# A latent attention layer: scaling on ScalarE, values absorbed, and a maximum in three ranges

## The chip, the cores and the metric

The kernel runs on one core of a Trainium2 chip. The metric is the device time of one execution in microseconds (us), as the median of the runs. TensorE multiplies, VectorE, ScalarE and GpSimd compute on tiles, SyncE (SP) issues DMAs. All order between them is made by semaphores that the kernel writes out by hand.

## The reference, cut to what matters

Two layers on 1024 tokens of width 1024. The change touches the mixer of the first, attention with a latent key and value of 128:

```
cq  = rmsnorm(h @ w_dq)                 # 1024 x 384
ckv = rmsnorm([h_ctx; h] @ w_dkv)       # 1280 x 128, 256 context rows first
q_nope, q_rope = cq @ w_uq              # 8 heads, 128 and 64 wide
k_nope, v      = ckv @ w_ukv            # 8 heads, 128 and 128 wide
k = [k_nope, rope(kr)];  q = [q_nope, rope(q_rope)]
p = softmax(q @ k.T / sqrt(192))        # per head 1024 x 1280
o = p @ v                               # per head 1024 x 128
y = o @ w_o
```

Both layers go on with a gated ConvFFN, and the second mixer is a Conformer convolution. All of it is float32.

## The kernel before, in words

Activations lie transposed, features in the partitions. A float32 product is made of three products of float32r parts: `three()` (L2061) multiplies low by high, high by low and high by high into one PSUM bank. So each operand is first split: ScalarE copies the value into a high part, VectorE subtracts this from the value to get the low part. Transposes and the folds of the rotary part are plain float32.

Attention runs in half-steps n = 0 to 17, two to a head: even n takes the first 512 queries of head n/2, odd n the others. A half-step has four query blocks s = 0 to 3 of 128 queries. For each, TensorE makes the scores against 1280 keys (`scores()`, fifteen products into PSUM banks 0 to 2, in the key ranges 512, 512 and 256 of `KP`), VectorE the maximum over 1280 columns and its negation (`maxes()`, L1582 and L1583), ScalarE the exponential with the row sum (`exps()`, L968), and VectorE the reciprocal and the scaling of the row of 1280 (`scales()`, L1589 and L1590). The next scores wait for `s_free`, which the exponential raises, as there is one set of score banks.

Behind each block of scores TensorE works on something else, by lists. `TURNS` gives the ten key blocks of the half-step before that are transposed (four transposes each, L2278; ScalarE and VectorE make high and low parts, `tp_copy` and `tp_sub`), `WEIGHS` the ten key blocks whose transposed probabilities are multiplied by the values (three products of 512 columns each, summed in bank 5), one half-step later still for the last three. `PIECES_AT` gives the pieces of the projections for a coming half-step: query parts ("q", nine products of 512), rotary parts ("qr", nine and two float32 folds), keys ("k", three products a range) and values ("v", three products of 128 columns for each key block, so 24 behind s = 2 and six behind s = 3 of an even half-step). Pieces take turns in banks 6 and 7; `pj_done` and `pj_free` count them, ten to a head.

Weights come by SP's queue in units of 128 x 1024, one a head: 768 columns for the queries, 128 for the keys, 128 for the values. In the second block of an even half-step ScalarE and VectorE split the next head's unit (`head_unit()`, L1577 on VectorE), VectorE before the maximum of the third block. When bank 5 is complete, ScalarE copies the head's 512 outputs to `OST` and issues a DMA of them to memory (`out_copy()`, L984). Later `heads_back()` (L1020) loads them again as input of the output projection; the last head's is loaded, and the third weight unit split, only when its store has landed. GpSimd sums the modulation vectors of the later sub-layers meanwhile, and TensorE finishes them with one-column products (L2097) behind the first scores of an even half-step, into bank 7.

n = 0, 1 and 14 to 17 are written out, n = 2 to 13 are a loop of three trips. n = 16 and 17 have no scores: they transpose and weigh what is left. Each engine's queue runs in the order in which `step()` issues it; nothing is reordered.

## Time and profile before

| | us |
|---|---|
| median of 3 runs (range) | 2547.52 (2545.29 to 2552.27) |
| the profiled execution | 2544.82 |
| its span in the trace | 2543.0 |
| TensorE busy | 2480.3 |
| VectorE busy | 1883.2 |
| ScalarE busy | 1150.0 |
| GpSimd busy | 933.3 |

The profile is of one execution. A row gives where an instruction begins (us from the span's start), how long it is busy, and, in brackets, how long its engine sat idle before it and what ended that. Matmuls are pipelined: the duration of one is longer than the distance to the next, so distances between starts are what count on TensorE, and rows that merge several instructions can hold waits. L numbers are lines of the kernel. Attention's half-steps lie between 139 and 672 us.

### The profile page before, as it was taken

The page shows a single profiled execution, that of the slowest core. Times are in us where ns is not written, and L with a number is a line of the kernel's source. Part 1 is how long each engine was busy: PE and PEld are TensorE (multiplying, and loading weights), DVE is VectorE, ACT ScalarE, POOL GpSimd, SP SyncE. Part 2 cuts the span into 40 slices and gives each one's busy share as a digit, 9 for nine tenths or more (in the row PEclk, how much of TensorE's full clock was granted, in tenths as well). Part 3 has the DMA queues.
Part 4 walks back from the last instruction along what each step waited for, and adds up shares of the span by engine and source line. Part 5 has one row for each costly group of instructions (what it writes and reads, how often), then busy time and mean ns, then how long its engine had stood idle before and what let it go on. Part 6 is the DMA issues. An engine that isn't in the chain of part 4 may idle for free.

```text
span 2543.0 us, 31195 instructions
## 1 busy us (share of the span) xinstructions
PE 2480.3 (98%) x11410; PEld 1998.7 (79%) x11410; DVE 1883.2 (74%) x2164; ACT 1150.0 (45%) x1821; POOL 933.3 (37%) x611
## 2 busy tenths in 40 slices
PE   7989999999899999999999999999999999999998
PEld 3868888888687788888888887756877888888876
DVE  5467776766547999999537379997689999994352
ACT  3334444444543555555435342235545555554331
POOL 0068685850043566564002010000445756630001
PEclk9999999999999999999999999999999999999999
DMA  6134333320431222223536320011212222236362
GB/s 264 35 108 133 100 116 107 124 82 17 173 109 58 76 83 79 88 83 108 203 115 199 113 92 34 34 46 54 100 59 78 80 91 84 76 107 224 125 198 75
DMA packets 101988, 262.38 MB, mean 103 GB/s; under 512 B 11104, under 2 KB 12384, under 8 KB 101856
## 3 DMA queue, kind: packets, MB, share of 16 engines
q1 hardware_dynamic: 86448, 209.65, 24.2%
q0 software_dynamic: 11520, 41.95, 5.1%
q10 hardware_dynamic: 3888, 9.05, 1.0%
q8 instruction: 80, 1.31, 0.2%
q14 instruction: 52, 0.43, 0.1%
HBM read 216.56 MB, written 44.04 MB: 102 GB/s over the span
## 4 chain that ended last, share of the span: by engine, by line
PE 79%; DVE 15%; issue 2%; DMA 1%; ACT 1%; POOL 0%; SPq 0%; POOLq 0%; ACTq 0%; DVEq 0%
PE psum L2064 24%; PE psum L2066 23%; PE psum L2065 23%; DVE acts L1974 3%; DVE acts L1976 3%; PE psum L2278 2%; PE psum L2268 1%; PE psum L2267 1%; DVE weights_f32r L1671 1%; DVE acts L1978 1%; PE psum L2097 1%; DMA low<-x_t 1%; DVE high_f32r L1792 1%; DVE small L1582 1%; PE psum L2364 1%
## 5 line engine op out<-in xcount | busy, mean ns | idle before, releaser
L2064 PE MATMUL psum<-acts_f32r,weights_f32r 128*128 128x512 f32 x1728 | 683.4, 396 | 10.5 <-DVE acts_f32r L1458 3.0
L2066 PE MATMUL psum<-acts_f32r,weights_f32r 128*128 128x512 f32 x1728 | 674.2, 390 | 0.0
L2065 PE MATMUL psum<-acts_f32r,weights_f32r 128*128 128x512 f32 x1728 | 674.0, 390 | 0.0
L761 POOL TENSOR_TENSOR low<-low 128x512 f32<-128x512 f32 x91 | 132.2, 1453 | 992.1 <-ACT low L1063 987.3
L844 ACT ACTIVATE weights_f32r<-low 128x512 fp32r<-128x512 f32 (+1 forms) x494 | 324.6, 666 | 334.1 <-PE psum L2066 242.1
L2064 PEld LDWEIGHTS psum<-acts_f32r,weights_f32r 128*128 128x128 f32 x1728 | 325.2, 188 | 81.3 <-issue 6.0
L1804 DVE TENSOR_TENSOR weights_f32r<-low,weights_f32r 128x512 fp32r<-128x512 f32 x264 | 380.1, 1484 | 0.1
L2066 PEld LDWEIGHTS psum<-acts_f32r,weights_f32r 128*128 128x128 f32 x1728 | 325.2, 188 | 68.8
L2065 PEld LDWEIGHTS psum<-acts_f32r,weights_f32r 128*128 128x128 f32 x1728 | 325.5, 188 | 67.9 <-issue 2.2
L1811 DVE TENSOR_TENSOR weights_f32r<-low,weights_f32r 128x512 fp32r<-128x512 f32 x176 | 125.6, 719 | 235.0 <-ACT weights_f32r L844 232.2
L788 POOL TENSOR_TENSOR low<-low 128x512 f32<-128x512 f32 x150 | 265.8, 1772 | 39.8 <-DVE acts_f32r L1789 29.3
L844 ACT ACTIVATE low<-psum 128x512 f32<-128x512 f32 (+2 forms) x246 | 147.6, 600 | 172.4 <-PE psum L2066 159.8
L2064 PE MATMUL psum<-high_f32r,weights_f32r 128*128 128x512 f32 (+1 forms) x464 | 184.5, 398 | 4.5 <-ACT low L844 4.5
L844 ACT ACTIVATE weights_f32r<-psum 128x512 fp32r<-128x512 f32 x160 | 92.9, 596 | 205.7 <-PE psum L2278 205.7
L2066 PE MATMUL psum<-high_f32r,weights_f32r 128*128 128x512 f32 (+1 forms) x464 | 179.2, 386 | 0.0
L2065 PE MATMUL psum<-high_f32r,weights_f32r 128*128 128x512 f32 (+1 forms) x464 | 179.2, 386 | 0.0
L811 POOL TENSOR_TENSOR low<-low 128x512 f32<-128x512 f32 x38 | 60.5, 1591 | 249.9 <-ACT low L844 249.9
L2064 PE MATMUL psum<-acts_f32r,high_f32r 128*128 128x256 f32 (+1 forms) x336 | 135.7, 404 | 10.8 <-ACT low L968 8.7
L1582 DVE TENSOR_REDUCE small<-psum 128x1 f32<-128x1280 f32 x64 | 95.3, 1490 | 60.4 <-PE psum L2268 60.0
L1156 ACT ACTIVATE low<-low,vectors 128x1024 f32<-128x1024 f32 x76 | 94.5, 1246 | 76.8 <-DVE low L1875 55.9
L738 POOL TENSOR_TENSOR set<-set 128x1024 f32<-128x1024 f32 x49 | 124.1, 2532 | 4.1
L2065 PE MATMUL psum<-acts_f32r,high_f32r 128*128 128x256 f32 (+1 forms) x336 | 125.3, 373 | 0.0
(240 smaller groups left out, 4646.7 us busy)
## 6 DMA issues: line engine op xcount, KB each, us to landing
low<-units SPq DMA_DIRECT2D x130, 512.0 KB, 4.1
low<-units SPq DMA_DIRECT2D x176, 256.0 KB, 3.5
set<-mod_w POOLq DMA_DIRECT2D x80, 512.0 KB, 3.9
gated<-low SPq DMA_DIRECT2D x44, 512.0 KB, 2.6
low<-gated SPq DMA_DIRECT2D x88, 256.0 KB, 4.0
residual<-low SPq DMA_DIRECT2D x48, 256.0 KB, 2.0
acts<-mod_w SPq DMA_DIRECT2D x4, 1024.0 KB, 8.9
low<-x_t SPq DMA_DIRECT2D x4, 1024.0 KB, 17.8
```

What stands on the lines that cost most here:

```text
L738: add = pool.tensor_tensor(acc, acc, part, ADD)
L761: pool.tensor_tensor(acc, first, ring(n), ADD).then_inc(sq_added, 1)
L788: pool.tensor_tensor(f(to[part - 1], HALF), x, y, op).then_inc(s_new, 1)
L844: return act.activation(out, in_, ACT.Copy, scale=scale)
L1156: act.activation(f(at), src, ACT.Identity, scale=V[:, wv + 2 * FB + c:wv + 2 * FB + c + 1], bias=V[:, wb + c:wb + c + 1]).then_inc(tap_mid, 1)
L1582: chain(dve.reduce_max(S[:, C_MX + c:C_MX + c + 1], PS[:, 0:KEYS], AX.X))
L1804: dve.tensor_tensor(r(at + HALF, HALF), src, r(at, HALF), SUB).then_inc(w_lo, 1)
L1811: dve.tensor_tensor(r(at + HALF, HALF), dn_raw(layer, dn_item(turn, j)), r(at, HALF), SUB).then_inc(w_lo, 1)
L1974: chain.lag(dve.scalar_tensor_tensor(out=into, in0=UE[i % 2][:, j:j + HALF + 1], scalar=tap(2 * j, i), in1=into, op0=MUL, op1=ADD))
L2064: pe.matmul(out, wl, xh, start=first, stop=False, skip_group_check=continued)
L2065: pe.matmul(out, wh, xl, start=False, stop=False, skip_group_check=continued)
L2066: return pe.matmul(out, wh, xh, start=False, stop=last, skip_group_check=continued)
```

## The change

Three things change together.

The values are absorbed. The probabilities are no longer multiplied by each head's values but by the latent itself, transposed once (`CT`, ten transposes in n = 0, copied and split by ScalarE and VectorE). The result, `weighed_at()`, is split again (ScalarE high, VectorE low), and an output piece "o" multiplies it by the head's value weights: three products of 512 columns behind s = 3 of an odd half-step (a head's second 512 queries), and six of 256 behind s = 2 of an even one (its first 512). VectorE copies the piece to `OST`, and SP, not ScalarE, stores it. The value weights are split apart from the rest of the unit, a half-step later than the next head's 896 other columns. Two weight units of the output projection are split in n = 16 instead of one.

The row is scaled by ScalarE (`normal()`, last in its turn for each block), and VectorE only makes the reciprocal.

The maximum is taken in three: TensorE raises `s_done` after each key range, and VectorE takes that range's maximum and combines it with the one before. Each of these five small or large instructions waits for the one ahead of it.

The numbers of pieces move with this (the scores of an odd half-step wait for eight instead of seven), and GpSimd's second accumulator moves.

```diff
@@ places: the accumulator, the transposed latent
-SPARE = 52736
+SPARE, MOD_ACC = 52736, 10240
-            return f(SPARE) if t % 3 == 1 else f(F_MD + 2 * L)
+            return f(MOD_ACC) if t % 3 == 1 else f(F_MD + 2 * L)
-        VS, KS = [R_V0, R_V1], [R_K0, R_K1]
+        KS = [R_K0, R_K1]
+        CT, CT_PS = R_V1, PS[:, 3 * HALF:3 * HALF + KEYS]
@@ the pieces and their places
-                  ("q", HALF, HALF), ("qr", HALF, HALF)] + [("v", a, n) for a, n in KP]
-        PIECES_AT = [[5], [6], [7, 8], [9]], [[0], [1, 2], [3, 4], []]
+                  ("o", 0, HALF), ("q", HALF, HALF), ("qr", HALF, HALF), ("o", 0, CTX), ("o", CTX, CTX)]
+        PIECES_AT = [[6], [7], [8, 9], []], [[0], [1, 2], [3, 4], [5]]
+        def value_w(slot, part, n):
+            return r(R_K0 + part * P, P) if isinstance(n, int) and n >= 2 * HEADS - 2 else w(slot, part, 7 * P, P)
+        def weighed_at(part, start=0, n=HALF):
+            return r(SPARE + part * HALF + start, n)
@@ SP
+            def store_out(n):
+                head, half = n // 2, n % 2
+                sp.wait_ge(pj_free, 10 * (head + 1 + half) + (6 if half else 10))
+                sp.dma_start(os_d[head, :, half * HALF:(half + 1) * HALF], OST[half]).then_inc(o_stored[half], 16)
-            load_units(U_HEAD, U_WO + 4)
+            load_units(U_HEAD, U_HEAD + 2)
+            for hd in range(HEADS):
+                sp.wait_ge(uv_lo, hd + 1)
+                load_units(U_HEAD + hd + 2, U_HEAD + hd + 3)
+                if hd:
+                    store_out(2 * hd - 2)
+                    store_out(2 * hd - 1)
+            load_units(U_WO + 2, U_WO + 3)
             sp.wait_ge(pj_free, 10 * HEADS)
             for v in range(2):
                 load_up(0, v)
+            store_out(2 * HEADS - 2)
+            load_units(U_WO + 3, U_WO + 4)
+            store_out(2 * HEADS - 1)
@@ ScalarE
-                elif u == U_WO + 1:
-                    act.wait_ge(pj_done, 10 * HEADS)
+                elif u in (U_WO, U_WO + 1):
+                    act.wait_ge(pj_done, 10 * HEADS + 5 + (u == U_WO))
+            def head_unit(head, c, i, n):
+                if not isinstance(n, int) or n < 2 * HEADS - 2:
+                    next_unit(head, c, i)
+                act.wait_ge(pj_done, 10 * head + 6)
+                copy(value_w(c % 2, 0, n), raw(c % 2)[:, 7 * P:]).then_inc(uv_hi, 1)
-                copy(w((c + 1) % 2, 0), raw((c + 1) % 2)).then_inc(w_hi, 1)
+                copy(w((c + 1) % 2, 0, 0, 7 * P), raw((c + 1) % 2)[:, 0:7 * P]).then_inc(w_hi, 1)
+            def normal(n, par, s):
+                c = (par % 2) * 4 + s
+                act.wait_ge(ri_ready, 4 * n + (s + 1))
+                copy(Pt(par, s), Pt(par, s), S[:, C_RI + c:C_RI + c + 1]).then_inc(p_ready, 1)
-            def out_copy(n, par, head):
+            def out_copy(n, par, i):
                 act.wait_ge(pt_free, NKB * n + (4 + NKB))
-                half = par % 2
-                act.wait_ge(o_stored[half], 16 * head + 16)
-                copy(OST[half], bank(5)).then_inc(o_free, 1)
-                act.wait_ge(o_free, n + 2)
-                act.dma_start(os_d[head, :, half * HALF:(half + 1) * HALF], OST[half]).then_inc(o_stored[half], 16)
+                act.wait_ge(pj_done, 10 * (2 * i + par // 2) + (6 if par % 2 == 0 else 10))
+                copy(weighed_at(0), bank(5)).then_inc(w_sum_hi, 1)
@@ ScalarE, step
+                    split(U_WO)
                     split(U_WO + 1)
...
                     if scored and s == 1 and par % 2 == 0:
-                        head_unit(head, c, i)
+                        head_unit(head, c, i, n)
+                    if scored:
+                        normal(n, par, s)
@@ VectorE
+                if kind == "o":
+                    dve.wait_ge(pj_done, 10 * head + (i + 1))
+                    half = int(i == 5)
+                    dve.wait_ge(o_stored[half], 16 * head - 16 * half)
+                    dve.tensor_copy(OST[half][:, start:start + width], piece_bank(i, width)).then_inc(pj_free, counts(n, i))
+                    return
-                dve.tensor_tensor(w(other, 1), raw(other), w(other, 0), SUB).then_inc(w_lo, 1)
+                if not isinstance(n, int) or n < 2 * HEADS - 2:
+                    dve.wait_ge(w_hi, U_HEAD + 2 + head)
+                    dve.tensor_tensor(w(other, 1, 0, 7 * P), raw(other)[:, 0:7 * P], w(other, 0, 0, 7 * P), SUB).then_inc(w_lo, 1)
+                dve.wait_ge(uv_hi, head + 1)
+                dve.tensor_tensor(value_w(c % 2, 1, n), raw(c % 2)[:, 7 * P:], value_w(c % 2, 0, n), SUB).then_inc(uv_lo, 1)
@@ VectorE, maxes and scales
-                dve.wait_ge(s_done, 4 * n + (s + 1))
-                chain(dve.reduce_max(S[:, C_MX + c:C_MX + c + 1], PS[:, 0:KEYS], AX.X))
-                dve.tensor_scalar(S[:, C_NM + c:C_NM + c + 1], S[:, C_MX + c:C_MX + c + 1], -SCALE, None, MUL).then_inc(s_max, 1)
+                best = C_MX + 3 * (s % 2)
+                for j, (at, width) in enumerate(KP):
+                    dve.wait_ge(s_done, 12 * n + (3 * s + j + 1))
+                    chain(dve.reduce_max(S[:, best + j:best + j + 1], PS[:, at:at + width], AX.X))
+                    if j:
+                        chain(dve.tensor_tensor(S[:, best + j:best + j + 1], S[:, best + j - 1:best + j], S[:, best + j:best + j + 1], ALU.max))
+                dve.tensor_scalar(S[:, C_NM + c:C_NM + c + 1], S[:, best + 2:best + 3], -SCALE, None, MUL).then_inc(s_max, 1)
-                chain(dve.reciprocal(S[:, C_RI + c:C_RI + c + 1], S[:, C_RS + c:C_RS + c + 1]))
-                dve.tensor_scalar(Pt(par, s), Pt(par, s), S[:, C_RI + c:C_RI + c + 1], None, MUL).then_inc(p_ready, 1)
+                dve.reciprocal(S[:, C_RI + c:C_RI + c + 1], S[:, C_RS + c:C_RS + c + 1]).then_inc(ri_ready, 1)
@@ VectorE, step
+                    if s == 0 and weighed:
+                        dve.wait_ge(w_sum_hi, n - 1)
+                        dve.tensor_tensor(weighed_at(1), bank(5), weighed_at(0), SUB).then_inc(o_free, 1)
...
+                    if isinstance(n, int) and n == 0 and s == 0:
+                        dve.wait_ge(ct_hi, 1)
+                        dve.tensor_tensor(r(CT + KEYS, KEYS), CT_PS, r(CT, KEYS), SUB).then_inc(ct_lo, 1)
@@ TensorE
-                if kind == "v":
-                    for b in range(width // P):
-                        at = start + b * P
-                        mm = three(out[:, b * P:(b + 1) * P], [r(R_CKV + p * KEYS + at, P) for p in range(2)],
-                                   [w(slot, p, 7 * P, P) for p in range(2)], True, True)
+                if kind == "o":
+                    back, done = outs
+                    if start == 0:
+                        pe.wait_ge(uv_lo, back + 1)
+                        pe.wait_ge(o_free, done)
+                    mm = three(out, [value_w((par - 1 - int(i == 5)) % 2, p, n - 2) for p in range(2)], [weighed_at(p, start, width) for p in range(2)], True, True)
...
                     mm = pe.matmul(PS[:, at:at + width], r(R_Q + 2 * L + q, P), r(R_KR + at, width), start=False, stop=True)
-                mm.then_inc(s_done, 1)
+                    mm.then_inc(s_done, 1)
...
-                vs, pt = VS[(par // 2) % 2] + kb * P, R_PT + (kbn % 4) * L
-                mm = three(bank(5), [r(vs + p * KEYS, P) for p in range(2)], [r(pt + p * HALF, HALF) for p in range(2)],
+                pt = R_PT + (kbn % 4) * L
+                mm = three(bank(5), [r(CT + p * KEYS + kb * P, P) for p in range(2)], [r(pt + p * HALF, HALF) for p in range(2)],
...
+                        if isinstance(n, int) and n == 0 and s == 0:
+                            for kb in range(NKB):
+                                mm = pe.transpose(CT_PS[:, kb * P:(kb + 1) * P], CKV[:, kb * P:(kb + 1) * P], ident[:, :])
+                            mm.then_inc(ct_done, 1)
```

Left out are the new semaphores, `counts()`, which makes the numbers of pieces come out at the ends, and the same calls with new arguments.

## Rows read from the trace of the kernel before

**Rows 1.** The page: the chain that ended last, by engine.

```profile
PE 79%; DVE 15%; issue 2%; DMA 1%; ACT 1%; POOL 0%; SPq 0%; POOLq 0%; ACTq 0%; DVEq 0%
```

**Rows 2.** Windows: length, busy us (instructions) by engine, clock, DMA.

```profile
216.80:608.50 391.70, 389.40 (x2180) 330.27 (x2179) 281.65 (x397) 176.55 (x294) 253.32 (x181) 0.99 0.31 99
```

**Rows 3.** Timeline of TensorE, half-step n = 4: start, us, instruction.

```profile
283.41 0.80 PE L2064 MATMUL psum<-acts_f32r,high_f32r 128*128 128x512 f32 x1
...
286.72 0.60 PE L2278 MATMUL psum<-ident,low 128*128 128x128 f32 x4
...
289.59 0.31 PE L2064 MATMUL psum<-weights_f32r,high_f32r 128*128 128x128 f32 x1
...
292.30 0.45 PE L2064 MATMUL psum<-acts_f32r,high_f32r 128*128 128x512 f32 x1
...
294.65 0.28 PE L2064 MATMUL psum<-acts_f32r,high_f32r 128*128 128x256 f32 x1
...
295.25 0.60 PE L2278 MATMUL psum<-ident,low 128*128 128x128 f32 x4
```

**Rows 4.** Timeline of all engines, odd half-step n = 5, fourth block.

```profile
325.63 0.60 PE L2278 MATMUL psum<-ident,low 128*128 128x128 f32 x4
325.83 1.49 DVE L1582 TENSOR_REDUCE small<-psum 128x1 f32<-128x1280 f32 x1 [0.33 <-PE psum L2268]
...
327.36 0.15 DVE L1583 TENSOR_SCALAR small<-small 128x1 f32<-128x1 f32 x1
...
327.46 1.40 PE L2278 MATMUL psum<-ident,low 128*128 128x128 f32 x8
327.55 1.33 ACT L968 ACTIVATE low<-psum,small 128x1280 f32<-128x1280 f32 x1 [0.68 <-DVE small L1583]
...
329.02 0.50 PE L2064 MATMUL psum<-acts_f32r,high_f32r 128*128 128x512 f32 x1 [0.16 <-ACT low L968]
```

**Rows 5.** Groups by form, head loop: count, busy us, mean ns, idle.

```profile
L1596 DVE TENSOR_TENSOR weights_f32r<-psum,weights_f32r 128x512 fp32r<-128x512 f32 x120 | 80.9, 686 | 15.6 <-ACT weights_f32r L844 15.4
...
L1590 DVE TENSOR_SCALAR low<-low,small 128x1280 f32<-128x1280 f32 x49 | 63.9, 1304 | 1.7
...
L1577 DVE TENSOR_TENSOR weights_f32r<-low,weights_f32r 128x1024 fp32r<-128x1024 f32 x6 | 12.3, 2050 | 1.0 <-ACT weights_f32r L844 0.9
...
L1570 DVE TENSOR_TENSOR acts_f32r<-psum,acts_f32r 128x256 fp32r<-128x256 f32 x12 | 4.9, 411 | 0.0
```

**Rows 6.** Timeline, n = 12: third scores begin; weight pass.

```profile
546.12 0.80 PE L2064 MATMUL psum<-acts_f32r,high_f32r 128*128 128x512 f32 x1
...
548.30 2.45 DVE L1577 TENSOR_TENSOR weights_f32r<-low,weights_f32r 128x1024 fp32r<-128x1024 f32 x1 [0.23 <-ACT weights_f32r L844]
```

**Rows 7.** Timeline of VectorE, n = 4: the same pass.

```profile
285.95 1.40 DVE L1577 TENSOR_TENSOR weights_f32r<-low,weights_f32r 128x1024 fp32r<-128x1024 f32 x1
```

**Rows 8.** Timeline of TensorE, n = 0: fourth scores.

```profile
161.04 0.79 PE L2064 MATMUL psum<-acts_f32r,high_f32r 128*128 128x512 f32 x1 [2.56 <-ACT low L968]
```

**Rows 9.** Windows: the 3 us behind it.

```profile
161.00:164.00 3.00, 2.96 (x7) 2.38 (x8) 2.25 (x4) 0.97 (x2) 2.57 (x4) 0.50 0.43 124
```

**Rows 10.** Timeline of TensorE, n = 4: column sums, next scores.

```profile
266.77 1.84 PE L2097 MATMUL psum<-ones,high 128*128 128x1 f32 x16
...
275.34 0.39 PE L2064 MATMUL psum<-acts_f32r,high_f32r 128*128 128x512 f32 x1
```

**Rows 11.** Timeline of TensorE, n = 8: column sums, next scores.

```profile
395.49 1.84 PE L2097 MATMUL psum<-ones,high 128*128 128x1 f32 x16
...
407.23 0.39 PE L2064 MATMUL psum<-acts_f32r,high_f32r 128*128 128x512 f32 x1
```

**Rows 12.** Timeline of TensorE in the tail.

```profile
652.29 0.63 PE L2278 MATMUL psum<-ident,low 128*128 128x128 f32 x4 [2.01 <-DVE weights_f32r L1596]
...
679.47 0.50 PE L2064 MATMUL psum<-acts_f32r,weights_f32r 128*128 128x512 f32 x1 [2.73 <-DVE acts_f32r L1606]
```

**Rows 13.** Timeline of ScalarE in the tail: split behind the store.

```profile
675.89 1.06 ACT L844 ACTIVATE weights_f32r<-low 128x1024 fp32r<-128x1024 f32 x1 [4.84 <-DMA heads_out<-set]
```

More of the change, by code:

```diff
@@ L1611, in step @@
                         if s == 0:
+                            split(U_WO)
                             split(U_WO + 1)
@@ L1625, in step @@
                     head, c = head_of(par, i)
-                    if scored and not (isinstance(n, int) and n == 2 * HEADS - 1):
-                        for p in PIECES_AT[par % 2][s]:
+                    for p in PIECES_AT[par % 2][s]:
+                        if active(p, n, scored, weighed):
                             turn_rotary(head, p)
@@ L1651, in _ @@
                 with dve.Fori(0, trips) as i:
-                    chain.enter(i, 32)
+                    chain.enter(i, 80)
                     for q in range(2, 6):
@@ L2211, in key_fold, with piece @@
                 mm.then_inc(kr_folded, 1)
-            def piece(head, par, i, mods=None, first=False):
+            def piece(head, par, i, mods=None, first=False, outs=None, n=-1):
                 slot = par % 2
@@ L2313, in step @@
                     head, c = head_of(par, i)
-                    pieces = PIECES_AT[par % 2][s] if scored and not (isinstance(n, int) and n == 2 * HEADS - 1) else []
+                    pieces = [p for p in PIECES_AT[par % 2][s] if active(p, n, scored, weighed)]
+                    outs = (out_head(par, i), n)
                     for p in pieces:
                         if PIECES[p][0] == "qr":
-                            piece(head, c, p, mods)
+                            piece(head, c, p, mods if p % 2 else None, n=n)
                     back = 2 if s == 0 else 1
@@ L2325, in step @@
                         if PIECES[p][0] != "qr":
-                            piece(head, c, p, mods)
+                            piece(head, c, p, mods if p % 2 else None, outs=outs, n=n)
                     if turns:
```

59 lines of the change are left out of this document (35 added, 24 removed).

## The prediction

> **What bounds the kernel now.** I read the page first, then the busy times by stretch, then TensorE's own timeline, and last the queues of VectorE and ScalarE around the gaps found there. The page has TensorE busy for 2480.3 of 2543.0 us (the table above), and the chain that ended last runs on it for 79% of the span, with VectorE at 15% [rows 1]. That is an average over all stages; the change touches only attention. There (216.8 to 608.5 us, the loop over the heads) TensorE is busy for 389.4 of 391.7 us, VectorE for 281.7, ScalarE for 176.6 [rows 2]. So the first reading is: every product taken from TensorE is time gained, and ScalarE has room.
>
> The second reading weakens this. In an odd half-step, last query block, the scores end at 325.63 and the next begin at 329.02, 3.39 us later, with only 0.16 us noted as idle [rows 4]; but eight transposes stand there in one row of 1.40 us, twice what transposes take elsewhere, so that row hides a wait. I listed all 64 blocks of scores: wherever little work stands between two of them the gap is 3.38 to 3.39 us (the fourth block of nearly every half-step, all three gaps of the last scored one, two of the first). That is a cycle, not work: the scores of the next query block need the same three PSUM banks, and those come free by maximum, then exponential. Its parts are in [rows 4]: hop 0.20, maximum over 1280 columns 1.49, gap 0.04, negated maximum 0.15, hop 0.04, exponential 1.33 and its sum, next scores 1.47 after the exponential began. In the other gaps TensorE's work decides. What the change is worth must therefore be read gap by gap.
>
> **The change, part by part.**
>
> *Values absorbed.* Each head loses 30 products of 128 columns: 24 behind the third query block of the even half-step take 2.71 us (289.59 to 292.30 [rows 3]), so the six behind the fourth 0.68. It gets three of 512 columns (0.23 us apart, 0.69) behind the fourth block of the odd half-step and six of 256 columns (five take 0.60 us, so 0.72) behind the third block of the even one [rows 3]. Plain subtraction: 3.39 - 1.41 = 2.0 us a head, 16 us in all.
>
> *The cycle with the maximum in three.* A maximum over 512 or 256 PSUM columns is not in the trace. Bounds for 512: 0.4 of 1.49 = 0.60 if all of it is per column, 0.60 + 0.15 if a one-element instruction's 0.154 is paid again; I take 0.69, what a 512-column VectorE pass over PSUM costs [rows 5]. For 256: 0.30 to 0.45, taken 0.41, same reason. The two comparisons are one-element instructions, 0.16 each. The last range's five products take 0.59 us, so counted from the end of the scores the second range's maximum runs from -0.39 to 0.30, its comparison to 0.50, the last maximum to 0.96, comparison to 1.17, negation to 1.36, where it ended at 1.88 before [rows 4]. The cycle becomes 2.87 us instead of 3.39: 0.52 gained where the cycle decides, nothing elsewhere. At the upper ends, and with a between-engine hop of 0.2 instead of 0.04 at each chained step, it is 3.4 and nothing is gained; at the lower ends 2.75.
> The Trainium skill (page VectorE: DVE Perf Modes, section The TRN2 errata) says that each instruction pays a fixed latency which splitting multiplies, and advises tiles of 512 or more; its table gives 0.66 and 0.39 us for such passes, as estimates. It speaks against the split, yet by its figures the cycle would be 0.05 shorter than mine.
>
> *Even half-step, fourth block (seven, n = 2 to 14).* Work left is three transposes and two weighings: the first transpose group and the weighings take 1.83 us (325.63 to 327.46 [rows 4]), two more groups 0.36 each, 2.55 us, under the cycle. 7 x 0.52 = 3.6 us, not the 0.68 each that the products cost.
>
> *Odd half-step, fourth block.* Here the new products fall in the wait: 2.55 + 0.69 = 3.24 us of work against 3.39. Gain 6 x 0.15 = 0.9.
>
> *Even half-step, third block.* TensorE alone would need 3.31 (scores) + 3.66 (the 5.58 of now, less 2.71, plus 0.72 and 0.07 for a restart) = 6.97 us instead of 8.89 [rows 3]. But VectorE is late: before the maximum it takes the low part of the next head's weights. That pass began 2.54 and 2.18 us after the scores (285.95 against 283.41, 548.30 against 546.12) and lasts 2.05 us on the mean of six, 2.45 in the second of these [rows 3, 5 to 7]. In the new kernel it is 7/8 as long (1.79), then comes a value part of 128 columns (0.28, estimate from 0.41 for 256), then all three ranges one behind another with nothing overlapped, 0.69 + 0.69 + 0.41 + 0.16 x 3 + 0.2 = 2.48 in place of 1.68, then 1.51 to the next scores. 2.36 + 1.79 + 0.28 + 2.48 + 1.51 = 8.42, so 0.47 gained instead of 1.92. Six half-steps: 2.8 us. At n = 14 there is no next unit: 1.9 us.
>
> *Scaling on ScalarE.* VectorE loses 0.89 to 3.1 us (mean 1.30 [rows 5]) a block, ScalarE gains one pass of 1280 columns: taken 1.33 as the exponential [rows 4], bounds 1.2 to 1.6. It stands last in each of ScalarE's turns. The transposes of the next half-step wait for it, but behind the next scores (3 us), and 0.16 + 0.6 + 1.33 fit. ScalarE goes from 45% to some 62% of this stretch. Inside the loop this costs nothing: the scores and transposes of TensorE cover it. Where that cover is gone, in the tail, it is counted. Sixteen output copies and DMA issues leave ScalarE for VectorE and SP; a low part of the weighted sum (0.69) comes to VectorE each half-step, beside TensorE's 2.5 to 6 us of other work before its bank is needed. The output products wait for the value's low part, a head old, and for that of the weighted sum, two blocks old; only behind the last weighing is that wait bare (tail). The stores on SP now wait for VectorE's copy, and behind them in SP's queue stand only loads needed a head later. GpSimd's partial sums only change their place: nothing.
>
> *Start (n = 0, 1).* The ten transposes of the latent and one piece fill the first gap (3.1). The copies of the transposed latent (1.33 on ScalarE, 1.5 to 1.7 on VectorE) stand before the second block's maximum and cost 0.8; the third block is held by the weight pass as now, the fourth gains 0.6, n = 1 gains 0.4 and 0.5. Together 1.5 gained.
>
> *n = 15.* Its first three gaps are cycles: 3 x 0.5 = 1.5.
>
> *Tail, a loss.* From the end of the last scores (647.10): ScalarE has one weight unit more to split (1.06) before its first copy, VectorE too (1.22), so the next TensorE work is 1.35 late; by the second turn this is 0.35, since ScalarE no longer waits for its own store. The output products (0.72) and their copies bring it to 0.7 when the last weighing ends at 670.4. Then the old kernel copied (0.60) and stored; the store took 4.3 us, and only then did ScalarE split the unit at 675.89 and TensorE resume at 679.47 after 2.73 us idle [rows 12, 13]. The new one puts low part 0.7, products 0.85 and copy 0.75 in between: 2.4 more. Tail 3.1 lost; 1.5 to 6 as bounds, the upper with ScalarE's pass at 1.6 and the DMA behind a unit load.
>
> **Sum.** 3.6 + 0.9 + 2.8 + 1.9 + 1.5 + 1.5 - 3.1 = 9.1 us. The profiled execution took 2544.82 (span 2543.0), so 2535.7; the median of the runs is 2.7 us above it, so I say 2538.
>
> **Rivals.**
> *B, the products come off in full.* If VectorE's weight pass is short (1.23 was seen, the shortest of the six), all seven third blocks gain 1.92: 13.4 instead of 4.7, 2529.5. For it: less VectorE work leaves room. Against: 2.05 is the mean, with GpSimd at work. The Trainium skill (SBUF — State Buffer, section Who interferes with whom) has a VectorE pass with two SBUF inputs blocked by a reading GpSimd instruction; this pass is one, and the change leaves it so. Chance 0.20.
> *C, VectorE and ScalarE take over.* Upper prices: third blocks gain 0 (-2.8), cycles 0.2 instead of 0.52 (-2.2 and -1.0), the start 0.5 (-1.0), the tail 1.5 worse. Gain 0.6: 2547, no change. For it: VectorE is late at the third blocks already. Against: it loses more busy time (1.30 a block) than it gets (some 0.8). 0.23.
> *D, the slower side: the clock.* At n = 0 TensorE idled 2.56 us before the fourth scores; the granted clock was 0.50, the 1.2 GHz level, in the 3 us behind [rows 8, 9]. It also fell behind 32 one-column products in one half-step: from their start to the next scores it took 11.74 us against 8.57 for the same work in another half-step [rows 10, 11], 3.2 lost. The change removes the products that covered VectorE's lateness, so in six even half-steps an idle of some 1.5 us on the mean (8.42 - 6.97) appears before the fourth scores. If each brings a fall: 6 x 3.2 = 19 lost, 2557. It decides from about three falls. Against: the idles of 2.01 and 2.73 us in the tail [rows 12] were followed by full clock. The Trainium skill (TensorE: Matmul & The Clock Gate, section What's actually happening) says that the slow state is the default which activity lifts. Chance 0.12.
>
> **How the numbers follow.** The forecast has 0.45, B 0.20, C 0.23, D 0.12. A difference under 0.3% (7.6 us) can't be told from none here. The forecast's own range is 2531 to 2544, about six tenths of it below 2539.9: 0.28, with B 0.48, rounded 0.49 faster. Same: 0.15 of it and C, 0.38. Slower: D and a rest, 0.13. Range 2526 to 2550: from under B to past C; only D lies outside.
>
> **What would show it.** Gaps behind the fourth block of even half-steps at 2.9 (right) or 3.3 (C); scores three to four of an even half-step 8.4 apart with VectorE releasing, or 7.0 (B); granted clock 1.00 through the loop but at n = 0 (not D); in the tail, TensorE resuming 35.5 us after the end of the last scores where it was 32.4. A shift outside attention would make it wrong altogether.

## The result, and the profile after

The changed kernel took 2602.76 us (median of 4 runs, 2599.22 to 2603.27), the kernel before beside it 2546.53 (4 runs): 1.022 times as long, 95% interval 1.020 to 1.024. The forecast was 2538.0, range 2526 to 2550. So 56 us were lost where 9 were expected to be gained. The span of the profiled execution is 2597.4 us, 54.4 more than before. From the first product of the first scores to the end of the last scores it went from 507.7 to 560.3 us, 52.6 of the 54.4; the scores began 3.1 later (nothing changed ahead of them; in other runs they began between 139.1 and 143.7), and behind them 1.3 us were saved, which is less than that part varies between the runs below (1894.5 to 1903.8 us).

The chain that ended last, by engine. To the row of [rows 1] answers:

```profile
PE 71%; DVE 20%; issue 4%; ACT 2%; DMA 2%; POOL 0%; ACTq 0%; SPq 0%; DVEq 0%; POOLq 0%
```

TensorE lost eight points of it, VectorE won five. Then the loop over the heads, of the changed kernel, as a window (length, then busy us and instructions of TensorE, its weight loads, VectorE, ScalarE, GpSimd, then clock, DMA share, GB/s):

```profile
215.19:651.31 436.12, 393.19 (x2053) 325.24 (x2053) 317.79 (x558) 228.41 (x331) 246.39 (x182) 0.96 0.27 91
```

In [rows 2] TensorE idled for 2.3 of 391.7 us; here for 42.9 of 436.1, and the clock fell to 0.96. VectorE was to be relieved, yet is busy for 318 us where it was for 282. Which of its instructions grew is seen in the groups by form (count, busy us, mean ns, idle before), changed kernel, most of the loop:

```profile
L1652 DVE TENSOR_TENSOR small<-small 128x1 f32<-128x1 f32 x90 | 68.3, 759 | 3.1
L1643 DVE TENSOR_TENSOR weights_f32r<-low,weights_f32r 128x128 fp32r<-128x128 f32 x6 | 14.9, 2480 | 0.0
L1641 DVE TENSOR_TENSOR weights_f32r<-low,weights_f32r 128x896 fp32r<-128x896 f32 x6 | 7.5, 1245 | 0.2
L1653 DVE TENSOR_SCALAR small<-small 128x1 f32<-128x1 f32 x45 | 6.9, 154 | 1.6
L1650 DVE TENSOR_REDUCE small<-psum 128x1 f32<-128x512 f32 x88 | 60.5, 688 | 24.6 <-PE psum L2345 17.0 <-issue 4.8
```

The comparisons (L1652) are one-element instructions as the negation (L1653) is, and take five times as long; the 128 columns of the value's low part (L1643) take twice what 896 columns do. The ranges (L1650) cost what was forecast. The reason is in the timeline of all engines, n = 4, third block, changed kernel (start, us, instruction, idle before; rows of other work left out):

```profile
306.82 0.79 PE L2140 MATMUL psum<-acts_f32r,high_f32r 128*128 128x512 f32 x1
...
308.92 1.27 DVE L1641 TENSOR_TENSOR weights_f32r<-low,weights_f32r 128x896 fp32r<-128x896 f32 x1
...
309.32 3.12 POOL L779 TENSOR_TENSOR set<-set 128x1024 f32<-128x1024 f32 x1
...
310.11 2.48 DVE L1643 TENSOR_TENSOR weights_f32r<-low,weights_f32r 128x128 fp32r<-128x128 f32 x1
...
312.62 1.51 DVE L1650 TENSOR_REDUCE small<-psum 128x1 f32<-128x512 f32 x2
...
313.38 1.13 POOL L778 TENSOR_SCALAR set<-set,small 128x1024 f32<-128x1024 f32 x1
...
314.15 0.37 DVE L1652 TENSOR_TENSOR small<-small 128x1 f32<-128x1 f32 x1
...
314.59 2.34 POOL L779 TENSOR_TENSOR set<-set 128x1024 f32<-128x1024 f32 x1
314.64 0.42 DVE L1650 TENSOR_REDUCE small<-psum 128x1 f32<-128x256 f32 x1
315.10 1.84 DVE L1652 TENSOR_TENSOR small<-small 128x1 f32<-128x1 f32 x1
316.98 0.15 DVE L1653 TENSOR_SCALAR small<-small 128x1 f32<-128x1 f32 x1
...
317.17 1.33 ACT L1016 ACTIVATE low<-psum,small 128x1280 f32<-128x1280 f32 x1 [5.80 <-DVE small L1653]
...
318.63 0.79 PE L2140 MATMUL psum<-acts_f32r,high_f32r 128*128 128x512 f32 x1 [4.69 <-ACT low L1016]
```

Add start and length to get the ends. The value's low part ends at 312.59, GpSimd's addition (L779) at 312.44. The first comparison ends at 314.52, GpSimd's scaling (L778) at 314.51. The second ends at 316.94, GpSimd's next addition at 316.93. Each of these VectorE instructions, which read two SBUF tensors, lasts until GpSimd's running instruction is over. It is so through the whole trace: of the 128 comparisons 60 took longer than 0.25 us, and all 60 end within 0.02 us behind the end of a GpSimd instruction, 29 times an addition, 31 times a scaling; the 128 take 0.69 us on the mean (0.76 in the stretch of the groups above). The maximum, which reads PSUM, passed beside GpSimd in its usual 0.42. TensorE then idled 4.69 us. And a second loss stood behind the first; the changed kernel's windows right behind that idle, and during the work ahead of it:

```profile
319.00:322.00 3.00, 3.00 (x8) 2.32 (x8) 2.04 (x4) 1.32 (x2) 2.82 (x2) 0.50 0.61 239
310.50:313.50 3.00, 3.00 (x20) 2.57 (x18) 2.85 (x3) 0.60 (x1) 2.66 (x3) 1.00 0.08 30
```

The granted clock was 0.50, the 1.2 GHz level, and the fourth scores took 5.41 us where they took 2.94 before (a block's end is taken 0.12 us behind the start of its last product).

I took both kernels apart by the starts of the 64 blocks of scores (length of the scores, and gap to the next). The 52.6 us are: third gaps of the six even half-steps of the loop +17.8; their second gaps +6.9; their fourth scores, at the half clock, +12.8; their fourth gaps +3.0; odd half-steps +5.6; n = 0 and 1 +12.1 (4.8 of it the clock, of which 1.6 in the very first scores, ahead of every comparison; g2 below, which has no comparisons, shows it too); the gaps with one-column products, which vary from run to run, and the other first gaps -1.8; n = 14 and 15 -3.8; some tenths elsewhere.

n = 14 and 15 are the control inside this very trace: GpSimd has nothing to do there. VectorE's timeline, n = 14, changed kernel:

```profile
664.98 0.16 DVE L1652 TENSOR_TENSOR small<-small 128x1 f32<-128x1 f32 x1
...
671.11 0.29 DVE L1643 TENSOR_TENSOR acts_f32r<-low,acts_f32r 128x128 fp32r<-128x128 f32 x1
```

These are the forecast's 0.16 and 0.28. In these half-steps the forecast came true: 6.98 us from third to fourth scores (6.97 worked out), cycles of 2.90, 3.06 and 2.90 (2.87).

### The profile page after: what moved, and what is told of

Its sections match the earlier page's. It is cut to its first block, busy times and chain, and to the rows that moved or that the text cites. A ratio compares the mean times of both kernels' runs of the same rounds, so it can differ in the third digit from the quotient of the medians.

```text
span 2597.4 us, 31481 instructions
## 1 busy us (share of the span) xinstructions
PE 2485.9 (96%) x11252; PEld 1994.4 (77%) x11252; DVE 1926.7 (74%) x2381; ACT 1220.3 (47%) x1870; POOL 924.1 (36%) x611
## 4 chain that ended last, share of the span: by engine, by line
PE 71%; DVE 20%; issue 4%; ACT 2%; DMA 2%; POOL 0%; ACTq 0%; SPq 0%; DVEq 0%; POOLq 0%
PE psum L2140 22%; PE psum L2142 21%; PE psum L2141 21%; DVE acts L2050 3%; DVE small L1652 3%; DVE acts L2052 3%; DVE small L1650 2%; PE psum L2355 1%; PE psum L2345 1%; PE psum L2344 1%; DVE weights_f32r L1747 1%; DVE acts L2054 1%; ACT weights_f32r L885 1%; DMA low<-x_t 1%; DVE high_f32r L1868 1%
## 5 line engine op out<-in xcount | busy, mean ns | idle before, releaser
L885 ACT ACTIVATE weights_f32r<-low 128x512 fp32r<-128x512 f32 (+2 forms) x501 | 325.1, 659 | 332.7 <-PE psum L2142 244.2
L2140 PE MATMUL psum<-high_f32r,weights_f32r 128*128 128x512 f32 (+1 forms) x485 | 191.6, 395 | 4.5 <-ACT low L885 4.5
L2140 PE MATMUL psum<-acts_f32r,high_f32r 128*128 128x256 f32 (+1 forms) x336 | 142.1, 423 | 48.5 <-ACT low L1016 45.7
L2142 PE MATMUL psum<-high_f32r,weights_f32r 128*128 128x512 f32 (+1 forms) x485 | 185.7, 383 | 0.0
L2141 PE MATMUL psum<-high_f32r,weights_f32r 128*128 128x512 f32 (+1 forms) x485 | 185.6, 383 | 0.0
L885 ACT ACTIVATE weights_f32r<-psum 128x512 fp32r<-128x512 f32 x160 | 93.0, 596 | 139.1 <-PE psum L2355 139.0
L1650 DVE TENSOR_REDUCE small<-psum 128x1 f32<-128x512 f32 (+1 forms) x192 | 115.1, 600 | 46.8 <-PE psum L2345 32.4
L1016 ACT ACTIVATE low<-psum,small 128x1280 f32<-128x1280 f32 x64 | 85.1, 1330 | 123.5 <-DVE small L1653 123.5
L1665 DVE TENSOR_TENSOR weights_f32r<-psum,weights_f32r 128x512 fp32r<-128x512 f32 x160 | 108.4, 689 | 44.5 <-ACT weights_f32r L885 44.0
```

The lines of the kernel that those rows point to most:

```text
L885: return act.activation(out, in_, ACT.Copy, scale=scale)
L1016: act.activation(Pt(par, s), PS[:, 0:KEYS], ACT.Exp, bias=S[:, C_NM + c:C_NM + c + 1], scale=SCALE, accum_out=S[:, C_RS + c:C_RS + c + 1]) ...
L1650: chain(dve.reduce_max(S[:, best + j:best + j + 1], PS[:, at:at + width], AX.X))
L1665: dve.tensor_tensor(r(at + HALF, HALF), bank(3 + kbn % 2), r(at, HALF), SUB).then_inc(tp_lo, 1)
L2140: pe.matmul(out, wl, xh, start=first, stop=False, skip_group_check=continued)
L2141: pe.matmul(out, wh, xl, start=False, stop=False, skip_group_check=continued)
```

## The experiments

Two theories. P: a VectorE instruction with two SBUF tensors waits for GpSimd's running instruction, and the comparisons, 128 of them, put this wait into the cycle. S: the split of the maximum itself costs this, through five chained instructions and three signals. Beside them V: the absorbed values and VectorE's load; and the clock, as a cause or a follower. The kernel before took 2545.89 us beside e1 to e4, 2549.11 beside f1 to f4, 2546.57 beside g1 to g3; ratios are against these. The edits are shown shortened: S[best+j] stands for the column S[:, best + j:best + j + 1], and "..." and plain words stand for code that is left out; counters that follow from an edit are not shown.

| kernel | median us | ratio (95% interval) | third gap | fourth scores | fourth gap |
|---|---|---|---|---|---|
| before | | 1 | 5.58 | 2.94 | 3.39 |
| changed | 2602.76 | 1.022 (1.020 to 1.024) | 8.55 | 5.07 | 3.88 |
| e1 comparison as tensor_scalar | 2548.05 | 1.0005 (0.999 to 1.002) | 5.43 | 3.47 | 2.98 |
| e2 one maximum | 2542.39 | 0.999 (0.997 to 1.000) | 5.06 | 3.49 | 3.38 |
| e3 GpSimd shortened | 2532.47 | 0.995 (0.993 to 0.996) | 4.24 | 2.99 | 3.04 |
| e4 before, with ranges | 2605.8 | 1.023 (1.020 to 1.026) | 9.96 | 5.04 | 3.38 |
| f1 e1, passes later | 2533.48 | 0.994 (0.992 to 0.996) | 3.67 | 2.88 | 3.87 |
| f2 f1, comparison fused | 2527.96 | 0.991 (0.989 to 0.993) | 3.67 | 2.88 | 3.55 |
| f3 before, ranges by tensor_scalar | 2565.33 | 1.007 (1.004 to 1.009) | 5.96 | 3.24 | 4.86 |
| f4 e1, scaling on VectorE | 2563.98 | 1.0065 (1.004 to 1.009) | 6.27 | 3.73 | 3.68 |
| g1 f2, value pass in the odd half-step | 2523.55 | 0.991 (0.990 to 0.993) | 3.67 | 2.88 | 3.00 |
| g2 before, scaling on ScalarE | 2550.23 | 1.001 (1.000 to 1.002) | 5.58 | 2.95 | 3.39 |
| g3 changed, GpSimd in halves | 2574.36 | 1.012 (1.009 to 1.014) | 6.36 | 4.13 | 3.90 |

The last three columns are means, in us, over the six even half-steps of the loop in the profiled execution.

**e1, the form of the comparison.**

```diff
-chain(dve.tensor_tensor(S[best+j], S[best+j-1], S[best+j], ALU.max))
+chain(dve.tensor_scalar(S[best+j], S[best+j-1], S[best+j], None, ALU.max))
```

> The changed kernel with one edit: the 128 one-element comparisons are made by tensor_scalar (the second maximum given as the per-partition scalar) instead of tensor_tensor; count, order and the waits between them stay. Theory P (a VectorE instruction with two SBUF tensors waits for the GpSimd instruction that is running, and the comparison is such a one): each comparison falls from 0.76 us on the mean to 0.16, the chain behind a block's scores returns to 1.4 us, and the time to 2546 to 2561; what is left over my forecast of 2538 is the 128-column low part of the values, 2.48 us, which still has two SBUF tensors. Theory S (the splitting itself, its fixed costs and the wait of each small instruction for the one before): nothing changes, 2600. Theory V (the absorbed values, their low part and the copies on VectorE): about 2595.

The same arithmetic with the second operand given as a per-partition scalar: 54.7 us less than the changed kernel. Its groups:

```profile
L1652 DVE TENSOR_SCALAR small<-small 128x1 f32<-128x1 f32 x103 | 22.1, 214 | 3.7
L1641 DVE TENSOR_TENSOR weights_f32r<-low,weights_f32r 128x896 fp32r<-128x896 f32 x5 | 7.3, 1458 | 0.6
L1643 DVE TENSOR_TENSOR weights_f32r<-low,weights_f32r 128x128 fp32r<-128x128 f32 x5 | 5.8, 1162 | 0.0
```

All 128 comparisons take 0.21 to 0.22 us, 63 of them begun while a GpSimd addition or scaling was running. The same place as above, timeline of e1, n = 4 (VectorE and GpSimd):

```profile
290.50 1.12 POOL L778 TENSOR_SCALAR set<-set,small 128x1024 f32<-128x1024 f32 x1
291.28 0.22 DVE L1652 TENSOR_SCALAR small<-small 128x1 f32<-128x1 f32 x1
...
291.71 2.34 POOL L779 TENSOR_TENSOR set<-set 128x1024 f32<-128x1024 f32 x1
292.08 0.21 DVE L1652 TENSOR_SCALAR small<-small 128x1 f32<-128x1 f32 x1
```

The weight passes are still held, and the third gap is still 5.43. Nothing is gained against before: the loss is gone, but the forecast's 9 us are not there.

**e2, one maximum again**, scaling and values as changed.

```diff
-for j, (at, width) in enumerate(KP): ...
+dve.wait_ge(s_done, 12 * n + (3 * s + 3))
+chain(dve.reduce_max(S[C_MX + c], PS[:, 0:KEYS], AX.X))
```

> The changed kernel with the maximum over all 1280 columns in one instruction again, as before; values absorbed and scaling on ScalarE stay. Theory P: 2550 to 2560: no comparison is left, but the cycle between blocks is 3.39 us again and the third blocks of even half-steps still wait for the low part of the values. Theory S: about the same. Theory V: 2595, as the cause is still in. Against e1 it tells whether a split without two-tensor comparisons is worth having: P expects e1 5 us faster.

This rules V out: the loss comes with the maximum in three, not with the values or the scaling. The time is under the 2550 to 2560 that P had given, and e1, which P expected 5 us faster than e2, is not faster (1.0005 against 0.999, the intervals overlap): with the passes where they are, the split brings nothing even in its cheap form.

**e3, GpSimd shortened.** This kernel leaves out most of the modulation sums of the later sub-layers, so its results are not the layer's; it serves for the time alone.

```diff
-chain(pool.tensor_scalar(part, part, ...)); add = pool.tensor_tensor(acc, acc, part, ADD)
+chain(pool.tensor_scalar(part[:, 0:8], ...)); add = pool.tensor_tensor(acc[:, 0:8], ...)
```

> The changed kernel with GpSimd's multiply and add passes over the modulation weights cut from 1024 to 8 columns (for all but the first weight block of each sum), its DMAs and waits kept; this leaves most of the modulation vectors of the later sub-layers out. VectorE's instructions are untouched. Theory P: every comparison takes 0.16 us and the low part of the values 0.28 us, the idle before the fourth blocks shrinks to under 1 us, and the time is 2528 to 2540. Theories S and V: 2595 or more, since VectorE's own work is the same.

VectorE's program is that of the changed kernel, tensor_tensor comparisons and all, and the loss turns into a gain. Groups:

```profile
L1652 DVE TENSOR_TENSOR small<-small 128x1 f32<-128x1 f32 x104 | 17.9, 172 | 3.6
...
L1643 DVE TENSOR_TENSOR weights_f32r<-low,weights_f32r 128x128 fp32r<-128x128 f32 x5 | 1.4, 287 | 0.0
```

This rules S out as the source of the 56 us. The time is near the forecast (2532.47 against 2538.0), which had priced the new instructions as if nobody held them; but the terms do not agree one by one. From the first to the end of the last scores e3 gains 20.2 us in its profiled execution where the sum had 12.2, the weight pass among them, which the forecast had taken at its held mean.

**e4, the ranges alone** in the kernel before.

```diff
-chain(dve.reduce_max(S[C_MX + c], PS[:, 0:KEYS], AX.X))
+for j, (at, width) in enumerate(KP): wait, reduce_max, and chain(dve.tensor_tensor(..., ALU.max)) if j
```

> The kernel before with one part of the change alone: the maximum in three ranges, with tensor_tensor comparisons, and a semaphore per range. Theory P: slower by 20 to 40 us, 2567 to 2587, with comparisons of 0.7 us on the mean. Theory V: no change or 5 us faster. Theory S: some 30 us slower too (it is told from P by e1 and e3).

The whole loss appears with this one part, and more than P had given for it (2567 to 2587): beside the comparisons the longer weight pass (next row) shows in it, and VectorE still scales the row here, to which f3 comes back. Groups, e4 (L1586 is the comparison, L1577 the weight pass of 1024 columns, 2050 in [rows 5]):

```profile
L1586 DVE TENSOR_TENSOR small<-small 128x1 f32<-128x1 f32 x87 | 60.0, 690 | 3.0
L1577 DVE TENSOR_TENSOR weights_f32r<-low,weights_f32r 128x1024 fp32r<-128x1024 f32 x6 | 18.0, 2996 | 0.2
```

**g3, the same GpSimd work in shorter instructions**, with the changed kernel's comparisons.

```diff
-add = pool.tensor_tensor(acc, acc, part, ADD)
+chain(pool.tensor_tensor(acc[:, 0:HALF], acc[:, 0:HALF], part[:, 0:HALF], ADD))
+add = pool.tensor_tensor(acc[:, HALF:], acc[:, HALF:], part[:, HALF:], ADD)
```

> The changed kernel, tensor_tensor comparisons as they are, but each of GpSimd's additions of 1024 columns made as two of 512, one behind the other. The work and its sum stay, only the running instruction is shorter. Theory P (a comparison waits for the end of GpSimd's running two-input instruction): the held comparisons take up to 1.3 us instead of up to 2.27, their mean falls from 0.76 to some 0.45, and about half of the 56 us of loss is left: 2570 to 2580. A rival (GpSimd's share of a port slows VectorE in proportion to its busy time): no change, 2600.

About half of the loss went (2574.36), so the length of the single GpSimd instruction sets the wait, not GpSimd's share of the time (it is busy for 64% of the loop here, 56% in the changed kernel); the mean comparison came down to 0.57 in the same stretch, less far than the 0.45 expected. Timeline of VectorE and GpSimd, g3, n = 4:

```profile
304.19 1.26 POOL L779 TENSOR_TENSOR set<-set 128x512 f32<-128x512 f32 x1
...
304.70 0.76 DVE L1653 TENSOR_TENSOR small<-small 128x1 f32<-128x1 f32 x1
...
305.53 1.27 POOL L780 TENSOR_TENSOR set<-set 128x512 f32<-128x512 f32 x1
...
311.69 1.12 POOL L778 TENSOR_SCALAR set<-set,small 128x1024 f32<-128x1024 f32 x1
...
312.05 0.77 DVE L1653 TENSOR_TENSOR small<-small 128x1 f32<-128x1 f32 x1
```

The first comparison ends at 305.46, as the running half does (305.45), and passes ahead of the other half. The second ends with GpSimd's scaling of one tensor (312.81), which holds it as well.

**f1, the weight passes behind the maximum**, comparisons as in e1.

```diff
-if scored and s == 1 and par % 2 == 0: head_unit(head, c, n)     # end of the second block's turn
+if s == 2 and par % 2 == 0: head_unit(*head_of(par, i), n)       # right behind maxes() of the third
```

> The changed kernel with the comparisons as tensor_scalar, and VectorE's two low parts of head weights (896 and 128 columns) taken behind the negated maximum of the third block of an even half-step, no longer ahead of that block's first range. With the scalar form alone the third gaps of the six even half-steps of the loop were 4.72, 6.71, 5.60, 4.33, 6.91 and 4.33 us, against 3.67 where TensorE's own work decides. If those gaps are two-input SBUF passes held by GpSimd (theory P): 3.7 to 4.0 each, 8 to 10 us less, and no fall of the clock behind them, another 3: median near 2536. If ScalarE (scaling and the split of the weights) holds the third block, as a rival has it: 4.2 at least, and no more than 5 us gained, 2543. If the late passes hold the reciprocal and with it the transposes: fourth gaps of the even half-steps above 3.1, nothing gained.

The third gaps are 3.67 in all six, TensorE's own work, so ScalarE, the rival there (4.2 at least), does not hold this block; the median is 14.6 us under e1's (17 by the ratios). But three of six fourth gaps are worse (3.70, 4.48, 5.91, the others 3.04): the held pass now keeps the transposes' low parts waiting. Timeline of VectorE, GpSimd and TensorE, f1, n = 6:

```profile
348.63 1.09 DVE L1641 TENSOR_TENSOR weights_f32r<-low,weights_f32r 128x896 fp32r<-128x896 f32 x1
...
348.82 3.15 POOL L779 TENSOR_TENSOR set<-set 128x1024 f32<-128x1024 f32 x1
349.64 2.48 DVE L1643 TENSOR_TENSOR weights_f32r<-low,weights_f32r 128x128 fp32r<-128x128 f32 x1
...
357.38 0.65 PE L2355 MATMUL psum<-ident,low 128*128 128x128 f32 x4 [1.25 <-DVE weights_f32r L1665]
```

**f2, one comparison fused with the negation.**

```diff
-compare behind range 2 and behind range 3, then tensor_scalar(nm, best+2, -SCALE, None, MUL)
+compare behind range 2 only, then tensor_scalar(nm, best+2, S[best+1], -SCALE, ALU.max, MUL)
```

> The kernel f1 with one comparison fewer in the chain behind the last range: maxima of the three ranges, the first two compared ahead of the third, and the last comparison made in one instruction with the negation (tensor_scalar with max and multiply). Behind the last range's maximum stands one one-element instruction instead of two. Theory P: where the cycle decides (fourth gaps of even half-steps and the gaps of n = 15, about ten gaps), 0.25 us less each, 3.02 to 2.8; 2 to 3 us less than f1. A rival has the cycle set by hops between engines that do not change with it: same as f1 within 0.5.

Where the cycle decides it is shorter: the gaps of n = 15 are 2.88, 3.00 and 2.87 (f1: 3.02, 3.07, 3.02). That is 0.07 to 0.15 a gap, not 0.25; the medians differ by 5.5 us, but the intervals overlap, and part of it is where the held pass fell.

**g1, the value's low part a half-step later.**

```diff
+if s == 1 and par % 2 and n != 15: value_low(head - 1, c - 1, n)   # behind maxes(), odd half-steps
```

> The kernel f2 with the value low part (128 columns, held up to 2.48 us) taken a half-step later, behind the negated maximum of the second block of the odd half-step, so that only the 896-column pass stays behind the third block's maximum of the even one. In f2 four fourth gaps of the even half-steps were 4.45, 4.65, 3.66 and 2.85 and two more 2.85: the late passes hold the transposes' low parts. If so: all near 2.85, 3 to 5 us less than f2 (2527.96), 2523 to 2525. A rival: the pass is held at its new place too and delays something there (second gap of odd half-steps, 5.91 in every kernel without held comparisons): as f2, 2528.

Four of the fourth gaps are 2.85, the others 3.17 and 3.43. This is the fastest version, 23 us below the kernel before beside it and 78 below the changed one by the two ratios; from f2 it can't be told with certainty (0.991 both). Its loop:

```profile
196.75:572.74 375.99, 375.44 (x2053) 317.64 (x2053) 256.70 (x511) 231.25 (x331) 259.75 (x194) 0.99 0.34 110
```

TensorE idles for 0.55 of 376.0 us: the loop is 15.7 us shorter than in [rows 2]. How much of that the split of the maximum earns is not known: one maximum with the passes behind it was not run.

**f3, f4 and g2, the scaling.** f3 is e4 with e1's comparison. f4 is e1 with VectorE scaling the row. g2 is the kernel before with ScalarE scaling it:

```diff
-chain(dve.reciprocal(ri, rs)); dve.tensor_scalar(Pt, Pt, ri, None, MUL).then_inc(p_ready, 1)
+dve.reciprocal(ri, rs).then_inc(ri_ready, 1)      # and on ScalarE, last in its turn: copy(Pt, Pt, ri)
```

> The kernel before with the maximum in three ranges and the comparisons as tensor_scalar; values and scaling as before. The same with tensor_tensor comparisons took 2605.8. Theory P (the form of the comparison, held by GpSimd, was the loss): the cycle goes from 3.39 to 3.05 in some 20 gaps, 7 us gained, less up to 0.8 at each of six third blocks where the ranges stand behind the weight pass: 2540 to 2546. Rival S (splitting the maximum costs by itself, through five chained instructions and TensorE's signals): 2560 or more.

> The changed kernel with the comparisons as tensor_scalar, and the row scaled on VectorE again. Beside the scalar form alone (2548.05) it tells what moving the scaling is worth. The prediction had nothing inside the loop: 2546 to 2550. A rival (V) has VectorE the late engine at the third block of even half-steps, where it now carries the low part of the weighed sum and the output's copy too: the scaling of 1.30 us ahead of the weight pass delays each third block, 6 x 1.3 = 8 us more, 2556.

> The kernel before with one edit: the row is scaled by ScalarE, last in its turn, and VectorE makes the reciprocal only. Maximum in one, values as before. In the changed kernel with scalar comparisons, moving the scaling back to VectorE cost 0.6% of the time, in the third and fourth gaps of even half-steps. If the scaling alone matters here too, it needs gaps that VectorE decides; before, the third gaps were 5.58 and the fourth 3.39, both set by TensorE or by the cycle: 2546 to 2550, no change (the prediction's view). Rival V: VectorE's load counts everywhere, 2535.

Moving the scaling alone is worth nothing (g2), as forecast: its third and fourth gaps are those of before. With the ranges it is worth 0.6% (f4 less e1, some 15 us), where f4's expectation had nothing, and its rival 8. f3 missed as well: I had expected 2540 to 2546, and 2565.33 lies where rival S had it (2560 or more). Of e4's loss the form of the comparison accounts for some 41 us (e4 less f3 by the ratios), and some 17 stay. The split by itself is not their cause, for e3 has the same split and gains; the trace points to the scaling. Groups, f3:

```profile
L1594 DVE TENSOR_SCALAR low<-low,small 128x1280 f32<-128x1280 f32 x44 | 60.5, 1374 | 1.8 <-DVE small L1593 0.3
...
L1577 DVE TENSOR_TENSOR weights_f32r<-low,weights_f32r 128x1024 fp32r<-128x1024 f32 x5 | 13.6, 2726 | 0.8 <-ACT weights_f32r L844 0.7
```

The scaling of the row is held by GpSimd too: 0.89 us alone, 1.75 beside a scaling of GpSimd's and 2.18 beside an addition, each ending 0.68 behind the end of that instruction. In the kernel before this delayed nothing (g2). With the ranges, VectorE is wanted 1.7 us before the scores end, when the first range is complete, and is late there: the fourth gaps grow from 3.39 to 4.86. That the held scaling makes f3's 17 us, and why the fourth gaps rather than the third take most of it, is read from the trace and from f4; f3 with a short GpSimd was not run, so it is not shown.

## Why the prediction was wrong

**The step that failed**: "The two comparisons are one-element instructions, 0.16 each". They took 0.69 on the mean of all 128, 0.76 in the loop, 2.27 at most. The price came from a one-element instruction with one input, the negation; the comparison has two tensors in SBUF. The value's low part, put at 0.28 as an estimate, failed for the same reason, 2.48 each. Both prices are right where GpSimd is idle (0.16 and 0.29 at n = 14), and e3 shows it for the whole kernel.

**The evidence was in hand.** I had listed the weight pass at 1.40 and 2.45 us in [rows 6, 7], twice the same 1024 columns, and the scaling from 0.89 to 3.1, and took means of them. What makes one instruction differ from its like by a factor should have been settled first: it held for every new instruction with the same operands, and the comparisons put 128 of these on the path, 60 of which were held. The Trainium skill (SBUF — State Buffer, section Who interferes with whom) says that a VectorE instruction with two SBUF inputs contends with a GpSimd instruction that reads SBUF; the forecast drew this on the weight pass alone, as a mark against rival B. By that rule the comparison is held as well, and the traces agree: 315.10 to 316.94 beside an addition that ends at 316.93. The Trainium skill has in the same section that tensor_scalar between SBUF tensors can contend too, since it may enter a mode that uses both ports. The row's scaling agrees (0.89 against 2.18 us); the one-element comparison in that form stayed at 0.21.

**Rival D came true as a second loss.** It was priced at 3.2 us a fall; the fourth scores lost 2.5 us at the full fall (5.41 against 2.94), 12.8 over six (two of them fell in part), and 3.2 in n = 0 and 1 behind the first scores. Its cause was as named, TensorE idle before the fourth scores, but idle 4.69 to 4.75 us at all six, not 1.5. The clock followed the wait and did not make it: e1, e3 and f1 change nothing on TensorE and have fewer or no falls there. It does not hang on the idle's length alone in these runs. f4, TensorE's timeline at the fourth scores of n = 2 and of n = 12, and the windows behind:

```profile
233.89 0.50 PE L2140 MATMUL psum<-acts_f32r,high_f32r 128*128 128x512 f32 x1 [3.06 <-ACT low L1016]
...
574.24 0.80 PE L2140 MATMUL psum<-acts_f32r,high_f32r 128*128 128x512 f32 x1 [3.03 <-ACT low L1016]
```

```profile
233.90:236.90 3.00, 3.00 (x16) 2.58 (x17) 2.96 (x5) 0.42 (x1) 2.87 (x3) 1.00 0.55 175
574.20:577.20 3.00, 2.96 (x7) 2.39 (x8) 2.95 (x5) 0.47 (x1) 2.87 (x3) 0.50 0.56 179
```

The same idle is followed by full clock once and by the half clock once, and in e2 an idle of 1.83 us (n = 4) by a fall, one of 2.50 (n = 10) by none. Filling the idle with other products, which would price the clock by itself, was not tried: all eight PSUM banks are in use there.

**What held.** The ranges cost 0.688 and 0.424 (0.69 and 0.41). The cycle is 2.90 (2.87), the odd fourth gap 3.32 (3.24), n = 14 in full. ScalarE's scaling takes 1.365 and hides. In the tail TensorE resumed 34.5 us after the end of the last scores, row below, where it was 32.4 and 35.5 was forecast; changed kernel, timeline of TensorE, to [rows 12]:

```profile
737.31 0.50 PE L2140 MATMUL psum<-acts_f32r,weights_f32r 128*128 128x512 f32 x1 [0.52 <-DVE acts_f32r L1675]
```

**What was off besides.** The even third block was called late by VectorE in the kernel before. It was not, and the prediction's own terms say so (2.36 + 2.05 + 1.68 + 1.51 = 7.60 us, under the 8.89 of then): the gap there is 5.58 with one or the other engine scaling (g2), TensorE's work. Once the products are gone VectorE does decide, 4.24 with GpSimd short (5.11 forecast) and 5.43 with it, and moving the pass gives the full 1.9 of rival B. Moving the scaling was put at nothing inside the loop; that holds alone (g2), but with the ranges it is worth some 15 us (f4), a gain that the sum has no term for.

## What to carry to other kernels

Price a new VectorE instruction by the rows of one with the same kinds of operands, and where such rows differ by a factor, find what runs beside the long ones before taking a mean. A one-element instruction on the critical cycle is not cheap if it reads two SBUF tensors beside a busy GpSimd: give one operand as a per-partition scalar, or fuse it into the instruction behind. When VectorE must be on time earlier, every pass of it that GpSimd can hold belongs behind that point, not ahead of it.

## What the runs showed of the hardware

- The hold ends with GpSimd's running instruction, whichever it is (addition of two tensors or scaling of one), and the waiting VectorE instruction goes ahead of GpSimd's next: all 60 held comparisons of the changed kernel and all 63 of g3 end within 0.02 us behind it. A larger held instruction ends later by what is left of it: the 128-column pass 0.15, the row's scaling 0.68.
- The hold begins before GpSimd's instruction shows in the trace. 17 of the 60 comparisons start 0.21 to 0.44 us ahead of the recorded start of GpSimd's scaling and last to its end (first two rows below, changed kernel, timeline); the one that starts 0.47 ahead passes in 0.16 (last two).

```profile
303.22 1.49 DVE L1652 TENSOR_TENSOR small<-small 128x1 f32<-128x1 f32 x1
303.56 1.13 POOL L778 TENSOR_SCALAR set<-set,small 128x1024 f32<-128x1024 f32 x1
...
330.91 0.16 DVE L1652 TENSOR_TENSOR small<-small 128x1 f32<-128x1 f32 x1
...
331.38 1.13 POOL L778 TENSOR_SCALAR set<-set,small 128x1024 f32<-128x1024 f32 x1
```

- The hold works both ways. An addition that starts while a weight pass of VectorE runs lasts 3.12 to 3.15 us instead of 2.40, 0.7 more (f1: it starts at 348.82, the pass ends at 349.72).
- tensor_scalar with a per-partition scalar costs 0.21 us for one element, with a constant 0.15, tensor_tensor unheld 0.16.
